# Who computes the low parts of the split output weights in a hybrid decoder trunk

## What is computed

```python
for l in range(2):
    h = x @ w_in[l]
    y_s5, y_moba, y_gdn = s5_mixer(...), moba_mixer(...), gdn_mixer(...)
    mix = concatenate([y_s5, y_moba, y_gdn]) @ w_out[l]
    x = layer_norm(ALPHA * x + mix)
    x = layer_norm(ALPHA * x + (swiglu(x) if l == 0 else moe_ffn(x)))

# inside gdn_mixer, per head and chunk of 64 tokens:
#   qkv = silu(causal_conv(qkv, conv_w))               4 taps a channel
#   sol = triangular_solve(eye + lmat, [v * beta, k * beta * exp(g)])
#   then a scan over the 4 chunks: v_new = u - w @ S; o = q @ S + attn @ v_new; S = S * decay + k.T @ v_new
```

## Time and profile before

| | us |
|---|---|
| median of 3 runs (lowest, highest) | 1591.35 (1590.88, 1593.33) |
| the profiled execution | 1589.88 |
| its span, first to last instruction | 1588.1 |
| busy: TensorE, VectorE, ScalarE, GpSimd | 1544.4, 1263.9, 935.0, 117.1 |
| mean granted TensorE clock | 0.996 |

### The profile page before, as it was taken

How to read it: one execution, slowest core, us unless ns; L and a number is a source line. 1 busy time by engine, 2 the same in 40 slices (tenths; PEclk the granted TensorE clock), 3 DMA queues, 4 the chain that set the end, 5 groups by cost and what they waited for, 6 DMA issues and landing times.

```text
span 1588.1 us, 23112 instructions
## 1 busy us (share of the span) xinstructions
PE 1544.4 (97%) x8892; PEld 1254.6 (79%) x8892; DVE 1263.9 (80%) x1211; ACT 935.0 (59%) x795; POOL 117.1 (7%) x138
## 2 busy tenths in 40 slices
PE   7998999999999899999999999999999999999996
PEld 6777688888787767888888888888888888888874
DVE  6997765444549786888888888888888888888996
ACT  1265153343206524777777777777777777777774
POOL 0012292000000401000000000000000000000200
PEclk9999999999999999999999999999999999999998
DMA  9412588784443035999999999999999999999993
GB/s 327 161 54 82 199 295 308 276 293 165 159 161 106 16 127 207 395 394 394 395 395 359 396 394 347 396 393 347 396 394 347 396 394 347 396 393 355 398 395 141
DMA packets 190453, 472.27 MB, mean 297 GB/s; under 512 B 7632, under 2 KB 11856, under 8 KB 189328
## 3 DMA queue, kind: packets, MB, share of 16 engines
q1 hardware_dynamic: 186352, 454.23, 77.0%
q0 software_dynamic: 3024, 13.42, 2.3%
q10 hardware_dynamic: 1008, 3.67, 0.6%
HBM read 463.43 MB, written 25.69 MB: 308 GB/s over the span
## 4 chain that ended last, share of the span: by engine, by line
PE 84%; DVE 10%; issue 3%; ACT 2%; DMA 1%; ACTq 0%; SPq 0%; DVEq 0%; POOLq 0%
PE ps L1680 45%; PE ps L1691 24%; PE ps L1651 5%; DVE arena L1081 2%; PE ps L1753 2%; DVE lo L1181 1%; PE ps L2096 1%; PE ps L2092 1%; PE ps L1658 1%; ACT hi L682 1%; DVE arena L1104 1%; DVE arena L1124 1%; DMA arena<-in_w_in 1%; PE ps L1992 0%; PE ps L1672 0%
## 5 line engine op out<-in xcount | busy, mean ns | idle before, releaser
L1181 DVE TENSOR_TENSOR lo<-arena,hi 128x2048 fp32r<-128x2048 f32 x378 | 868.9, 2304 | 205.0 <-ACT hi L682 204.1
L682 ACT ACTIVATE hi<-arena 128x2048 fp32r<-128x2048 f32 x378 | 723.7, 1919 | 356.6 <-PE ps L1680 224.7
L1680 PE MATMUL ps<-hi,xg 128*128 128x512 f32 x1760 | 543.5, 390 | 0.6 <-DVE lo L1181 0.2
L1680 PEld LDWEIGHTS ps<-hi,xg 128*128 128x128 f32 x1760 | 329.1, 188 | 71.1 <-DVE lo L1181 3.5
L1680 PE MATMUL ps<-lo,xg 128*128 128x512 f32 x880 | 342.5, 389 | 0.0
L1691 PE MATMUL ps<-hi,hTe 128*128 128x512 f32 x896 | 282.4, 396 | 0.0
L1680 PEld LDWEIGHTS ps<-lo,xg 128*128 128x128 f32 x880 | 165.2, 188 | 34.5
L1691 PEld LDWEIGHTS ps<-hi,hTe 128*128 128x128 f32 x896 | 164.1, 188 | 31.9
L1691 PE MATMUL ps<-lo,hTe 128*128 128x512 f32 x448 | 175.1, 391 | 0.0
L1680 PE MATMUL ps<-hi,xs 128*128 128x512 f32 x512 | 159.8, 393 | 3.0 <-issue 1.9
L1651 PE MATMUL ps<-arena 128*128 128x256 f32 x544 | 121.8, 386 | 3.1 <-DMA arena<-in_w_in 2.1
(11 more groups left out here) (383 smaller groups left out, 1307.1 us busy)
## 6 DMA issues: line engine op xcount, KB each, us to landing
arena<-in_mg SPq DMA_DIRECT2D x112, 1024.0 KB, 7.7
arena<-in_mu SPq DMA_DIRECT2D x112, 1024.0 KB, 8.2
arena<-in_md SPq DMA_DIRECT2D x112, 1024.0 KB, 7.4
arena<-in_w_in SPq DMA_DIRECT2D x7, 2048.0 KB, 9.2
arena<-in_wg SPq DMA_DIRECT2D x14, 1024.0 KB, 5.2
arena<-in_wu SPq DMA_DIRECT2D x14, 1024.0 KB, 5.2
arena<-in_wd SPq DMA_DIRECT2D x14, 1024.0 KB, 5.4
xg_rows<-in_zeros SPq DMA_DIRECT2D x17, 512.0 KB, 7.3
```

Of the source, the lines that this page charges most:

```text
L682: af(hi[r % PARTS][:, :], raw[r % RAWS], ACT.Copy).then_inc(hi_ready, 1)
L1181: tt(lo[r % PARTS][:, :], raw[r % RAWS], hi[r % PARTS][:, :].bitcast(F32), ALU.subtract)\
L1680: ins = mm(ps[:, (4 if w == "G" else 4 + nb) + b, :], tok[a][:, kk * nt + b * P:kk * nt + (b + 1) * P], tiles_of(part[r % PARTS], w)[:, k, ...
```

## The change

- `WO_POOL` and `WO_DVE` become `WO_EARLY` (4, 5, 6) and `WO_REST` (7, 0, 1, 2, 3). All eight low parts are VectorE's: one behind each group of round 3, five ahead of the scan. One semaphore counts them.
- GpSimd has only masks. The mask of v = 3 waits, besides the products A of round 0, for the first evacuation of round 1 (`xy_used`).
- The taps of channel 7 stand behind groups 1 and 2 of round 0 (two each) instead of all four behind group 2. The taps of channel 8 stand in round 2 instead of round 1.
- ScalarE's table load stands behind the evacuation n = 8 instead of before n = 7, the Silu behind n = 10 instead of n = 7.
- The up products come in two parts: the heads 0, 1, 2 and 4 after 14 signals of `xy_used`, the heads 3 and 5 after 15.

```diff
-WO_POOL, WO_DVE = (4, 5, 6, 7, 0), (1, 2, 3)
+WO_EARLY, WO_REST = (4, 5, 6), (7, 0, 1, 2, 3)
...
                     if v > 2:
                         pool.wait_ge(a_psum, 15 * l + 3 * (v - 2))
+                    if v == 3:
+                        pool.wait_ge(xy_used, 15 * l + 4)
                     pool.tensor_tensor(M[v % 2], LA[:, :, 1, :],
                                        C(f"lv{v}").unsqueeze(1).to_broadcast([P, 12, CH]), ALU.mult)\
                         .then_inc(m_ready, 1)
-
-                pool.wait_ge(part_hi, 4 * l + 2)
-                for q in WO_POOL:
-                    own = slice(512 * q, 512 * (q + 1))
-                    pool.tensor_tensor(wo_parts[1][:, own], slot(2)[:, own], wo_parts[0][:, own].bitcast(F32),
-                                       ALU.subtract).then_inc(wo_lo, 1)
...
                     if n == 6:
                         act.wait_ge(pv_psum, l + 1)
                         af(mix_parts[1][0][:, :], ps[:, 4, :], ACT.Copy).then_inc(part_hi, 1)
+                    if n == 8:
                         act.preload_act_table_set("silu_and_others")
-                    if n == 7:
+                    if n == 10:
                         act.wait_ge(conv_v, l + 1)
                         af(qkv[:, 6:9, :], qkv[:, 6:9, :], ACT.Silu).then_inc(silu_done, 1)
...
+                def low_weights(q):
+
+                    own = slice(512 * q, 512 * (q + 1))
+                    dve.wait_ge(part_hi, 4 * l + 2)
+                    tt(wo_parts[1][:, own], slot(2)[:, own], wo_parts[0][:, own].bitcast(F32), ALU.subtract)\
+                        .then_inc(wo_lo, 1)
...
-                        if v < 2:
-                            for w in (((), (), (0, 1, 2, 3)), ((0, 1), (2,), (3,)))[v][g]:
-                                tap(l, 7 + v, w)
+                        if v == 3:
+                            low_weights(WO_EARLY[g])
+                        if v in (0, 2):
+                            for w in ((), (0, 1), (2, 3))[g] if v == 0 else ((0, 1), (2,), (3,))[g]:
+                                tap(l, 7 + v // 2, w)
...
-                dve.wait_ge(part_hi, 4 * l + 2)
-                for q in WO_DVE:
-                    own = slice(512 * q, 512 * (q + 1))
-                    tt(wo_parts[1][:, own], slot(2)[:, own], wo_parts[0][:, own].bitcast(F32), ALU.subtract)\
-                        .then_inc(wo_lo_rest, 1)
+                for q in WO_REST:
+                    low_weights(q)
...
-                pe.wait_ge(xy_used, 15 * (l + 1))
+                pe.wait_ge(xy_used, 15 * (l + 1) - 1)
                 pe.wait_ge(a_evac, 15 * (l + 1))
                 pe.wait_ge(kv_evac, 4 * (l + 1))
-                for b in range(NB):
-                    for h in range(NH):
...
+                for late in range(2):
+                    if late:
+                        pe.wait_ge(xy_used, 15 * (l + 1))
+                    for b in range(NB):
+                        for h in ((0, 1, 2, 4), (3, 5))[late]:
...
                         if k == 2:
-                            pe.wait_ge(wo_lo, len(WO_POOL) * (l + 1))
+                            pe.wait_ge(wo_lo, 8 * l + 4)
                         if k == 0:
-                            pe.wait_ge(wo_lo_rest, len(WO_DVE) * (l + 1))
+                            pe.wait_ge(wo_lo, 8 * (l + 1))
```

More of the change, by code:

```diff
@@ L320, in build @@
         wo_used, part_hi, wo_lo = sem("wo_used"), sem("part_hi"), sem("wo_lo")
-        wo_lo_rest = sem("wo_lo_rest")
         x_loaded = [sem(f"x_loaded_{b}") for b in range(NB)]
@@ L2053, in _ @@
                         probabilities(4, 5)
-                pe.wait_ge(xy_used, 15 * (l + 1))
+                pe.wait_ge(xy_used, 15 * (l + 1) - 1)
                 pe.wait_ge(a_evac, 15 * (l + 1))
                 pe.wait_ge(kv_evac, 4 * (l + 1))
-                for b in range(NB):
-                    for h in range(NH):
[L2060 to L2065, removed]
+                for late in range(2):
[3 more added lines that the diff above has]
+                        for h in ((0, 1, 2, 4), (3, 5))[late]:
+                            i = 6 * (h % 2) + 2 * (h // 2) + b
+                            for c in range(2):
+                                rows = chunk_rows(c)
+                                ins = mm(ps[rows, (2, 5)[b], h * HD:(h + 1) * HD], U[rows, i, :],
+                                         kv[rows, 1, b, h * HD:(h + 1) * HD], start=True, stop=True)
+                        if late:
+                            ins.then_inc(up_psum_, 1)
                 pe.wait_ge(kg_ready, NB * (l + 1))
```

## The result

Over 20 runs each, in turn on the same chips, the changed kernel took 1594.79 us (median; 1590.64 to 1596.92) and the kernel before 1591.55 us (1590.0 to 1594.64). The ratio is 1.0019, with a 95% interval of 1.0012 to 1.0025: slower by 3 us, at the bound of 0.2%. The range of the prediction, 1590.0 to 1595.6, holds it; the predicted 1593.2 is 1.6 us short.

What follows compares the result with a forecast made beforehand. TensorE was taken to bound the kernel (84% of its chain of waits). Per layer -0.40 + 0.30 + 0 + 1.06 = +0.96 us, +1.9 in all: profiled 1591.8, plus 1.47 to the median, forecast 1593.2 us; range 1590.0 to 1595.6.

Steps and rivals of the forecast that it cites:

- Round 1, -0.40: Earlier channel 7 taps free VectorE sooner, but product A of round 2 then waits for the third mask: -0.40 us a layer.
- Rival 2: Third mask in time, so TensorE keeps round 1's whole 2.4 us: -1.04 us a layer, 1589.3 us; chance 0.09.
- Round 2, +0.30: Channel 8 taps held by GpSimd's last mask, so round 3's first evacuation starts later: +0.30 us a layer.
- rival 1: Round 2's taps pass the mask without being held: +0.66 us a layer, 1592.6 us; chance 0.15.
- Round 3, 0: Three low parts on VectorE in round 3 fit its idle gaps: 0 us, bounds 0 and +1.8.
- Rival 3: Round 3's low parts delay evacuations TensorE waits for: +2.8 us a layer with the rest, 1596.9 us; chance 0.15.
- Ahead of the scan, +1.06: Five low parts instead of three on VectorE before the scan's first subtraction: +1.06 us a layer.
- The up products in halves: Two thirds move ahead of the last evacuation; TensorE reaches the scan 0.5 us or more earlier but waits for VectorE: 0.
- The sum, +0.96 a layer: All parts of the change added over the block inversion and the scan's opening: +0.96 us a layer, +1.9 us in all.
- A delay at the stretch's end goes into the end one to one: Delay after block inversion and scan's opening lengthens the kernel equally, since back-to-back TensorE matmuls and TensorE's expert stage follow.
- any difference of the two layers: Sign that the prediction is wrong: the layers differ beyond the delay handed on; layer 0 was worked out and doubled.

Runs made afterwards that it cites:

- e1_mask_free: The changed kernel, but GpSimd's mask of v = 3 no longer waits for the first evacuation of round 1; 1589.98 us, 0.9987 of the kernel before.
- e4_five_ahead: The kernel before, but GpSimd makes low parts 4, 5, 6 and VectorE the other five ahead of the scan; 1594.36 us, 1.0019 of the kernel before.
- e3_filler: The changed kernel with useless transposes on TensorE before its waits for round 2's mask (13) and the scan's first subtraction (9); 1591.95 us, 1.0006 of before.

## Why the prediction was right, and where it fell short

**Round 1, -0.40.** Measured -0.35 (b: 13.13 to 12.78). (The 2.44 us named there as TensorE's longest wait is the longest of this stretch; at start-up it waits 4.8 us for a DMA.) The mechanism was the right one: TensorE waits for the mask, and e1_mask_free shows the 2.0 us that this wait throws away. Rival 2, which had the mask in time, is what that experiment makes of it: 1590 us, where I had 1589.3.

**Round 2, +0.30.** Measured +0.27 in layer 0: from the last evacuation of round 1 to the first of round 3 it is 6.64 us (126.35 to 132.99) where it was 6.37, from 127.86 to this row of VectorE's timeline before:

```profile
134.23 0.42 DVE L1364 TENSOR_TENSOR arena<-arena,ps 128x256 f32<-128x256 f32 x1
```

In layer 1 it is +0.16. The TENSOR_SCALAR took 0.76 us beside the mask, where the text had said 0.75. It ended 0.15 us behind the mask, as the sum has it, but the text took that number from the held tap of the earlier trace rows, which ended 0.28 behind as it says itself: a figure with no source that came true. So a one-input TENSOR_SCALAR on SBUF is held like the two-input tap; rival 1 is out. The Trainium skill ("SBUF — State Buffer", the reading of its diagram) has the port pair locked against a one-input VectorE operation if it runs in a two-port mode. The trace agrees if this one does; which mode it ran in no run here shows. What I did not see is that the same taps cost 0.66 us, not 0.30, against the place in round 1 that mask and attention leave free: I compared with the kernel before, where they cost something too.

**Round 3, 0.** No TensorE wait there fell on a low part; the gap before the third group shrank from 1.02 to 0.24 us, and the third low part pushed the first evacuation of round 4 by 0.6 us, all of which VectorE's idle time behind it took up: the second came 5.07 us after the first of round 3 where it had come after 5.08. Rival 3 did not come, but the gap shows how near it was.

**Ahead of the scan, +1.06.** Measured +0.98 (from c to d, 5.29 to 6.27), and the same in e4_five_ahead by itself, where the two more low parts are all there is. The up products in halves brought TensorE to the scan early, and it waited 1.49 us there: nothing gained, as forecast.

**The sum, +0.96 a layer.** Measured 0.90 in layer 0, and in layer 1 0.79 without its stretch, 0.72 in e3_filler (31.12 to 31.84). The steady change is 1.6 to 1.7 us where 1.9 was forecast.

**What failed is a term that the sum did not have.** "A delay at the stretch's end goes into the end one to one", and the text took TensorE's time at full clock for granted, since the one profile showed 1.00 in both windows, which end ahead of the scan. A wait of TensorE is dearer than its length here, since half clock may follow it: 1.6 to 1.7 us each time. The medians rose by 3.2 us, and the forecast of 1.9 has no part of the other half. The steady part alone would have met the forecast (1591.55 + 1.7 = 1593.2). That the range held the rest too is luck: its upper end was drawn for low parts on the path, of which there were none. The test named in the text, "any difference of the two layers", is the one that came out wrong. That idle waits make these stretches more frequent is shown by the two fillers together (e3_filler, 2 to 3 us faster with the path unchanged, and 2.3 us less lost by its mean clock) and by the count over the 14 profiles; that the change makes them more frequent, by 0.9 us in the mean with a standard error of 0.4. What decides in which execution a wait costs the clock, and why layer 0's attention never lost it, stays open.

## What to carry to other kernels

Work that is moved from GpSimd to VectorE is paid where VectorE is waited for: with five low parts instead of three ahead of the scan 0.98 us a layer was lost, and with only two there and the rest in the gaps that the timeline of VectorE shows, 1.46 us a layer was won against five. Before adding a wait that keeps an instruction of one engine from being held by another's, price both: in round 0 being held cost 0.02 us, the wait 2.0 (in round 2, where taps met a mask on the path, 0.66). And where TensorE hops between short waits, look at the granted clock in more than one execution, since a profile without a half-clock stretch does not show that the kernel has none.

## What the runs showed of the hardware

- VectorE's one-input TENSOR_SCALAR, float32 in SBUF, 0.35 us alone, took 0.76 to 0.78 beside a GpSimd TENSOR_TENSOR and ended 0.15 to 0.2 us behind it; in the same timelines TENSOR_TENSORs of 128x256 with one operand in PSUM kept their 0.41 to 0.42 us.
- The granted clock fell to half for about 3.4 us in a mixer, in some executions, behind waits of TensorE of 1.5 to 2.4 us, and 0 to 2 us after TensorE had gone back to work. It cost 1.6 to 1.7 us. The same code with the same waits kept its clock in another execution.
- Useless transposes in TensorE's waits made the changed kernel 2 to 3 us faster (2.8 by the medians, 2.1 by the ratios), and the mean granted clock rose from 0.9937 to 0.9951. They do nothing but keep it busy.
